# One operation of 2048 columns in place of two of 1024 on VectorE, in the expert stage of a two-layer transformer block

## The chip, the cores and the metric

The kernel runs on one core of one Trainium2 chip. The metric is the device time of one execution in microseconds (us). All products are made on the matmul engine (PE); VectorE is called DVE, ScalarE ACT, GpSimd POOL and SyncE SP. PEld is PE's weight load, a track of its own in the trace.

## The reference

Two transformer layers run one after the other on 256 tokens of width 2048. The stage of interest is the second layer's `peer`: each token picks 16 of 16384 experts in each of 8 heads, takes the product of its input with each chosen row of a first table (`expert_u`), and adds up the rows of a second table (`expert_v`) with the resulting weights.

```python
    kk = PEER_HEADS * PEER_TOPK
    xt = xn.reshape(nblk, PEER_TOK_BLOCK, D)
    it = eidx.reshape(nblk, PEER_TOK_BLOCK, kk)
    gt = gates.reshape(nblk, PEER_TOK_BLOCK, kk)

    def block(args):
        xb, ib, gb = args
        act = jax.nn.gelu(jnp.einsum('tkd,td->tk', expert_u[ib], xb))
        return jnp.einsum('tk,tkd->td', act * gb, expert_v[ib])
```

## The kernel before

**How the stage computes.** The kernel does most tokens densely: 224 of the 256 tokens are multiplied by all 16384 rows of both tables, and the weights of the experts that a token didn't choose are zero. The other 32 tokens (`ROWS`) fetch their chosen rows. For each of 32 numbers c, one indirect DMA of POOL (`gather`, L2187) brings 128 rows of the first table into one of three buffers `rows`, and DVE multiplies them by the tokens and sums (the list `SUM`, L2516). Later 32 more gathers bring rows of the second table, and DVE adds them, each times its weight, into `row_sum` (the list `ADD`, L2527 for c = 0 and L2529 after that; `row_sum` and `row_tokens` in the trace are one tensor).

**Pieces and steps.** Weights arrive as pieces of 128x2048 fp32 (1 MB). PE multiplies in fp32r, so each piece is split into a rounded part, `weights_hi`, and the rest that the rounding left, `weights_lo`. ACT makes `weights_hi` in two halves of 128x1024 (`split_hi`, L188), and DVE makes `weights_lo` as the piece minus `weights_hi` (`split_lo`, L195), likewise in two halves, each of which waits for its own half of `weights_hi`. PE starts a piece when all of its `weights_lo` is there (`ring.wait`). There are two buffers each of `weights_hi` and `weights_lo`, so ACT may start on piece n when PE has finished piece n - 2, that is, while PE works on piece n - 1. The raw pieces lie in four slots. SP fills a slot (L148) when DVE has finished the `weights_lo` of the piece that was in it.

The stage counts its pieces as steps s. Steps 0 to 15 are the query weights, 16 to 143 the first table (PE lines L2231 and L2232), 144 to 271 the second table (L2286 and L2287), and 16 further steps belong to the matrix after it. `V0` is 144. Below, "step V0+33" is the step in which ACT and DVE split the piece 33 of the second table. Each engine walks through the steps in a program order written out by hand. In a step s from V0 on, DVE does, in this order:

- `weights_lo` of piece s;
- a row operation, if s is in `ADD`;
- `normed` times the tokens' scale (L2535, 128x1792), in the two steps of each 16 ahead of those in the list `CURVE`;
- eight evacuations of PE's sums (`leave_sums`, L2469), every 8th step. ACT has copied the other half of each (`spill_sums`, L2347) just before;
- the addition of these sums to the residual (`add_sums`, L2478), every 8th step;
- a subtraction of the list `SPLIT` (L2552, 128x448), after ACT's copy of the same list (L2410);
- a product of the list `PROD` (L2560, 128x448).

`SPLIT` and `PROD` are made of offsets within a group of 16 steps; both have an entry at V0+16g+1 and at V0+16g+13. PE begins the first piece of every eight (V0+8k) only when `leave_sums` has emptied the first bank, and goes on bank by bank.

**The row operations before.** Each gathered row set is handled in two halves of 1024 columns, in two different steps. `SUM` holds the 64 steps 78 to 141, and `ADD` 64 steps from V0+17 on that leave out the offsets 0, 5, 6, 8, 10 and 14 of each 16. The gather that reuses a buffer waits until both halves are done (`row_summed`).

Of the kernel before, what the change touches and what calls it, by code (L numbers as in the profile page):

```python
# [6 lines left out]
F32 = mybir.dt.float32  # L7
# [3 lines left out]
ALU = mybir.AluOpType  # L11
# [6 lines left out]
D = 2048  # L18
# [88 lines left out]
class Ring:  # L107
# [82 lines left out]
    def split_lo(self, dve, stream, i, j, half, skip=0):  # L190

        hi, lo, raw = self.piece(self.hi, half, stream), self.piece(self.lo, half, stream), self.raw(j, half, stream)
        for part, (k, n) in enumerate(self.parts_of(stream)):
            dve.wait_ge(self.hi_ready, i * 16 + (2 * (2 * (self.fills + j) + half) + part + 1))
            last = dve.tensor_tensor(lo[:, k, n], raw[:, k, n], hi[:, k, n].bitcast(F32), ALU.subtract)  # L195
        last.then_inc(self.lo_ready, 1 + skip)

# [29 lines left out]
class Kernel:  # L227
    WQ, ROWS, ZEROED = 384, 32, 8
# [1687 lines left out]
    def peer(self, stream):  # L1916
        nc, a, ring = self.nc, self.a, self.ring
        U0, V0, END = PQ_TILES, PQ_TILES + NKEYS, PQ_TILES + 2 * NKEYS
# [3 lines left out]
        ROWS, BUFS = self.ROWS, 3  # L1922
        SUM = [*range(78, 142)]
        DOTS = SUM[-1] + 1
        free = [s for s in range(V0 + 17, V0 + 118) if (s - V0) % 16 not in (0, 5, 6, 8, 10, 14)]
        ADD = [free[k * len(free) // (2 * ROWS)] for k in range(2 * ROWS)]
# [31 lines left out]
        with ExitStack() as ctx:  # L1958
# [41 lines left out]
            row_sum = xg  # L2000
# [134 lines left out]
            with self.block() as block:  # L2135
# [306 lines left out]
                def _(dve):  # L2442
# [40 lines left out]
                    for s in range(END):  # L2483
# [3 lines left out]
                        ring.split_lo(dve, tiles, i, j, half)  # L2487
# [23 lines left out]
                        for k in [k for k, at_step in enumerate(SUM) if at_step == s]:  # L2511
                            c, part = divmod(k, 2)
                            if part == 0:
                                dve.wait_ge(gathered[c % BUFS], 16 * (c // BUFS + 1))
                            row, x_row = [y[:, part * D // 2:(part + 1) * D // 2] for y in (rows[:, c % BUFS, :], xg)]
                            dve.tensor_tensor_reduce(row, row, x_row, 1.0, 0.0, ALU.mult, ALU.add, dots[:, part, c:c + 1])\  # L2516
                                .then_inc(row_summed, 1)
                        for k in [k for k, at_step in enumerate(ADD) if at_step == s]:
                            c, part = divmod(k, 2)
                            if part == 0:  # L2520
                                dve.wait_ge(gathered[(ROWS + c) % BUFS], 16 * ((ROWS + c) // BUFS + 1))
                            row, to = [y[:, part * D // 2:(part + 1) * D // 2] for y in (rows[:, (ROWS + c) % BUFS, :], row_sum)]
                            weight = row_gate[:, 0, c:c + 1]
                            if c > 0 or part > 0:
                                dve.wait_ge(row_summed, 2 * ROWS + max(k - 1, 0))
                            if c == 0:
                                last = dve.tensor_scalar(to, row, weight, None, ALU.mult)  # L2527
                            else:
                                last = dve.scalar_tensor_tensor(out=to, in0=row, scalar=weight, in1=to, op0=ALU.mult, op1=ALU.add)  # L2529
                            last.then_inc(row_summed, 1)  # L2530
# [6 lines left out]
                        if s == DOTS:  # L2537
                            dve.wait_ge(row_summed, 2 * ROWS)
                            dve.tensor_tensor(row_gate[:, 1, :], dots[:, 0, :], dots[:, 1, :], ALU.add).then_inc(row_scores, 1)
# [527 lines left out]
```

## Time and profile before

| what | value |
|---|---|
| median of 3 runs | 2959.6 us (2958.5 to 2960.16) |
| the profiled execution's own time | 2959.44 us |
| its span in the trace | 2957.7 us |
| PE busy | 2910.0 us, 98% |
| DVE busy | 1969.9 us, 67% |
| ACT busy | 1388.9 us, 47% |
| POOL busy | 593.0 us, 20% |
| granted PE clock | 0.998 of full |

The span is the profiler's, from the first to the last instruction; the execution's own time is 1.7 us longer. The busy share of an engine is a mean over stages with different loads: the table above doesn't tell which engine another one waits for. The profile's lists of waits and its timelines do.

### The profile page before, as it was taken

To read this page: it belongs to the slowest core of one execution; us is meant where nothing else is said; L and a number is where in the kernel's file an instruction comes from. 1 tells how busy PE (TensorE), PEld (TensorE's weight loads), DVE (VectorE), ACT (ScalarE), POOL (GpSimd) and SP (SyncE) were. 2 spreads that over 40 slices of the span, in tenths; PEclk is the share of its full clock that TensorE was granted. 3 is DMA by queue.
4 is the path that set the end of the run, shared out by engine and by line. 5 is a ranking of instruction groups with operands and counts; after the bars stand their busy time and mean duration, and the time that the engine had idled before them with its cause. 6 is when DMAs were issued, how large, how long until landed. Compare 5 with 4: busy or idle time off the path is not lost.

```text
span 2957.7 us, 41749 instructions
## 1 busy us (share of the span) xinstructions
PE 2910.0 (98%) x16599; PEld 2625.5 (89%) x16599; DVE 1969.9 (67%) x2753; ACT 1388.9 (47%) x1992; POOL 593.0 (20%) x555
## 2 busy tenths in 40 slices
PE   8999999999999999999999999999999999999999
PEld 7998778888888887978789999999999999999999
DVE  5556654444444445464568999677787888888876
ACT  4355544444444444354444444444455555555553
POOL 2000000000000000150004888488710000000000
PEclk9999999999999999999999999999999999999999
DMA  8554356666665554544567888899997888888764
GB/s 292 162 168 151 115 175 222 224 234 231 226 197 183 187 198 140 176 153 156 177 218 252 226 224 224 279 328 336 343 375 266 314 324 323 324 316 316 260 215 141
DMA packets 244456, 692.88 MB, mean 234 GB/s; under 512 B 46569, under 2 KB 98825, under 8 KB 210880
## 3 DMA queue, kind: packets, MB, share of 16 engines
q1 hardware_dynamic: 194560, 600.81, 59.4%
q0 software_dynamic: 47168, 86.54, 10.5%
q10 hardware_dynamic: 2560, 3.21, 0.4%
q8 instruction: 115, 1.88, 0.3%
q14 instruction: 53, 0.43, 0.0%
HBM read 654.70 MB, written 33.69 MB: 233 GB/s over the span
## 4 chain that ended last, share of the span: by engine, by line
PE 49%; DVE 2%; ACT 0%; issue 0%; ACTq 0%; DVEq 0%
PE banks L2231 16%; PE banks L2286 15%; PE banks L2232 8%; PE banks L2287 7%; PE banks L2307 1%; PE banks L2309 1%; PE banks L2308 1%; DVE weights_lo L195 1%; PE banks L2250 0%; DVE peer_features L376 0%; DVE top_index L2049 0%; ACT weights_hi L188 0%; PE banks L2259 0%; PE banks L2275 0%; DVE row_gates L2063 0%
## 5 line engine op out<-in xcount | busy, mean ns | idle before, releaser
L195 DVE TENSOR_TENSOR weights_lo<-weights,weights_hi 128x1024 fp32r<-128x1024 f32 (+4 forms) x1080 | 1228.4, 1179 | 702.8 <-ACT weights_hi L188 700.7
L188 ACT ACTIVATE weights_hi<-weights 128x1024 fp32r<-128x1024 f32 (+4 forms) x1080 | 1046.5, 1017 | 1370.6 <-PE banks L417 639.7
L2231 PE MATMUL banks<-peer_features,weights_hi 128*128 128x448 f32 (+1 forms) x2304 | 734.8, 378 | 6.1 <-DVE weights_lo L195 6.1
L415 PE MATMUL banks<-weights_hi,features_hi 128*128 128x512 f32 (+3 forms) x1600 | 608.0, 380 | 26.2 <-DVE weights_lo L195 23.0
L2232 PE MATMUL banks<-peer_features,weights_lo 128*128 128x224 f32 (+1 forms) x2304 | 610.2, 265 | 0.0
L417 PE MATMUL banks<-weights_hi,features_lo 128*128 128x512 f32 (+3 forms) x1600 | 602.5, 377 | 0.0
L416 PE MATMUL banks<-weights_lo,features_hi 128*128 128x512 f32 (+3 forms) x1600 | 602.4, 377 | 0.0
L2286 PE MATMUL banks<-peer_features,weights_hi 128*128 128x448 f32 x1568 | 492.5, 374 | 0.0
L2231 PEld LDWEIGHTS banks<-peer_features,weights_hi 128*128 128x128 f32 x2304 | 432.0, 187 | 48.6 <-DVE weights_lo L195 8.7
L2232 PEld LDWEIGHTS banks<-peer_features,weights_lo 128*128 128x128 f32 x2304 | 439.2, 191 | 0.0
L2197 POOL DMA_INDIRECT expert_gates<-peer_choice x224 | 399.4, 1783 | 182.3 <-DVEq L2071 102.8
L2287 PE MATMUL banks<-peer_features,weights_lo 128*128 128x224 f32 x1568 | 414.6, 264 | 0.0
L415 PEld LDWEIGHTS banks<-weights_hi,features_hi 128*128 128x128 f32 x1600 | 302.6, 189 | 76.3 <-issue 25.3
L416 PEld LDWEIGHTS banks<-weights_lo,features_hi 128*128 128x128 f32 x1600 | 303.1, 189 | 44.8 <-issue 0.2
L417 PEld LDWEIGHTS banks<-weights_hi,features_lo 128*128 128x128 f32 x1600 | 302.4, 189 | 45.3
L2286 PEld LDWEIGHTS banks<-peer_features,weights_hi 128*128 128x128 f32 x1568 | 294.2, 188 | 22.0
L2287 PEld LDWEIGHTS banks<-peer_features,weights_lo 128*128 128x128 f32 x1568 | 299.7, 191 | 0.0
L268 POOL TENSOR_SCALAR statistics<-statistics 128x2 f32<-128x2 f32 (+3 forms) x16 | 6.8, 428 | 799.3 <-DVE statistics L393 502.7
L2286 PE MATMUL banks<-applied_parts,weights_hi 128*128 128x448 f32 x480 | 152.7, 374 | 0.0
L2187 POOL DMA_INDIRECT expert_rows<-in_expert_v,attention_statistics x32 | 34.3, 1073 | 553.3 <-DVE row_tokens L2529 422.7
L415 PE MATMUL banks<-weights_hi,ffn_turned_hi 128*128 128x512 f32 x352 | 137.9, 392 | 0.0
L417 PE MATMUL banks<-weights_hi,ffn_turned_lo 128*128 128x512 f32 x352 | 137.4, 390 | 0.0
(400 smaller groups left out, 2729.3 us busy)
## 6 DMA issues: line engine op xcount, KB each, us to landing
weights<-in_expert_u SPq DMA_DIRECT2D x128, 1024.0 KB, 6.3
weights<-in_expert_v SPq DMA_DIRECT2D x128, 1024.0 KB, 6.4
weights<-in_w_ffn_gate SPq DMA_DIRECT2D x44, 1024.0 KB, 5.2
weights<-in_w_ffn_up SPq DMA_DIRECT2D x44, 1024.0 KB, 5.2
weights<-in_w_ffn_down SPq DMA_DIRECT2D x44, 1024.0 KB, 4.8
weights<-in_w_in SPq DMA_DIRECT2D x48, 900.0 KB, 5.0
weights<-in_w_out SPq DMA_DIRECT2D x32, 1024.0 KB, 5.1
weights<-in_w_in SPq DMA_DIRECT2D x24, 704.0 KB, 4.2
```

The lines of the kernel that those rows point to most:

```text
L188: act.activation(hi[:, k, n], raw[:, k, n], ACT.Copy).then_inc(self.hi_ready, 1 + skip)
L195: last = dve.tensor_tensor(lo[:, k, n], raw[:, k, n], hi[:, k, n].bitcast(F32), ALU.subtract)
L415: pe.matmul(out, xh, wh, start=first, stop=False)
L416: pe.matmul(out, xh, wl, start=False, stop=False)
L417: return pe.matmul(out, xl, wh, start=False, stop=last_one)
L2187: pool.indirect_dma_start(out=rows[:, c % BUFS, :], out_offset=None, in_=rows_d if c < ROWS else values_d, in_offset=bass.IndirectOffsetOn ...
L2197: pool.indirect_dma_start(out=g_rows[:, :], in_=gates_of[:, t, slot:slot + 1], in_offset=None, compute_op=ALU.add, out_offset=bass.Indirec ...
L2231: pe.matmul(self.bank(n % 3, 2 * cols), wh[:, k, :], F[:, k, :, 0:cols], start=(k == 0), stop=False)
L2232: last = pe.matmul(self.bank(n % 3, cols), wl[:, k, :], F[:, k, 0, 0:cols], start=False, stop=(k == KD - 1))
L2286: pe.matmul(both, wh[:, e, cols], applied_pair[:, e], start=(pair == 0 and e == 0), stop=False)
L2287: last = pe.matmul(self.bank(c, DENSE), wl[:, e, cols], applied_pair[:, e, 0], start=False, stop=(pair == 7 and e == 1))
L2307: pe.matmul(out, wh[:, k, cols], F[:, kk, 0, :], start=(kk == 0), stop=False)
```

## The change

Three things change, all on DVE, and nothing else in the program:

- From V0 on, `weights_lo` is made in one operation of 128x2048 (`split_lo_whole`), which waits for both halves of `weights_hi`. The steps before V0, and the 16 steps after the second table, keep the two halves.
- Each gathered row set is handled in one operation of 2048 columns. `SUM` is now every second step from 78 to 140. `ADD` has 32 steps, those in which the first halves stood. The semaphore `row_summed` counts two for each operation, so POOL's gathers wait for the same numbers.
- The partial dot products are no longer two to be added; a copy stands where the addition was.

```diff
+    def split_lo_whole(self, dve, stream, i, j, half):
+
+        hi, lo, raw = self.piece(self.hi, half, stream), self.piece(self.lo, half, stream), self.raw(j, half, stream)
+        dve.wait_ge(self.hi_ready, i * 16 + (2 * (2 * (self.fills + j) + half) + 2))
+        dve.tensor_tensor(lo, raw, hi.bitcast(F32), ALU.subtract).then_inc(self.lo_ready, 1)
...
-        SUM = [*range(78, 142)]
-        DOTS = SUM[-1] + 1
+        SUM = [*range(78, 142, 2)]
+        DOTS = SUM[-1] + 2
         free = [s for s in range(V0 + 17, V0 + 118) if (s - V0) % 16 not in (0, 5, 6, 8, 10, 14)]
-        ADD = [free[k * len(free) // (2 * ROWS)] for k in range(2 * ROWS)]
+        ADD = [free[k * len(free) // ROWS] for k in range(ROWS)]
...
-                        ring.split_lo(dve, tiles, i, j, half)
+                        if s < V0:
+                            ring.split_lo(dve, tiles, i, j, half)
+                        else:
+                            ring.split_lo_whole(dve, tiles, i, j, half)
...
+                        for c in [c for c, at_step in enumerate(SUM) if at_step == s]:
+                            dve.wait_ge(gathered[c % BUFS], 16 * (c // BUFS + 1))
+                            row = rows[:, c % BUFS, :]
+                            dve.tensor_tensor_reduce(row, row, xg[:, :], 1.0, 0.0, ALU.mult, ALU.add, dots[:, 0, c:c + 1])\
+                                .then_inc(row_summed, 2)
+                        for c in [c for c, at_step in enumerate(ADD) if at_step == s]:
+                            dve.wait_ge(gathered[(ROWS + c) % BUFS], 16 * ((ROWS + c) // BUFS + 1))
+                            row, weight = rows[:, (ROWS + c) % BUFS, :], row_gate[:, 0, c:c + 1]
+                            dve.wait_ge(row_summed, 2 * (ROWS + c))
                             if c == 0:
-                                last = dve.tensor_scalar(to, row, weight, None, ALU.mult)
+                                last = dve.tensor_scalar(row_sum[:, :], row, weight, None, ALU.mult)
                             else:
-                                last = dve.scalar_tensor_tensor(out=to, in0=row, scalar=weight, in1=to, op0=ALU.mult, op1=ALU.add)
-                            last.then_inc(row_summed, 1)
+                                last = dve.scalar_tensor_tensor(out=row_sum[:, :], in0=row, scalar=weight, in1=row_sum[:, :],
+                                                                op0=ALU.mult, op1=ALU.add)
+                            last.then_inc(row_summed, 2)
...
-                            dve.tensor_tensor(row_gate[:, 1, :], dots[:, 0, :], dots[:, 1, :], ALU.add).then_inc(row_scores, 1)
+                            dve.tensor_copy(row_gate[:, 1, :], dots[:, 0, :]).then_inc(row_scores, 1)
```

With the edited formula, `ADD` holds these offsets from V0: 17, 19, 23, 27, 29, 33, 35, 39, 43, 45, 49, 51, 55, 59, 61, 65, 67, 71, 75, 77, 81, 83, 87, 91, 93, 97, 99, 103, 107, 109, 113 and 115. Seven of them are of the form 16g+1 and six of the form 16g+13.

The order of DVE's instructions from the `weights_lo` of step V0+32 to that of step V0+35, in the kernel before:

```order
L195 TENSOR_TENSOR weights_lo<-weights,weights_hi 128x1024 x2
L2469 TENSOR_TENSOR peer_scratch<-banks,peer_scratch 128x224 x8
L195 TENSOR_TENSOR weights_lo<-weights,weights_hi 128x1024 x2
L2529 SCALAR_TENSOR_TENSOR row_tokens<-expert_rows,row_gates,row_tokens 128x1024
L2552 TENSOR_TENSOR peer_features<-normed,peer_features 128x2x224
L2560 TENSOR_TENSOR normed<-normed,peer_scratch 128x448
L195 TENSOR_TENSOR weights_lo<-weights,weights_hi 128x1024 x2
L2529 SCALAR_TENSOR_TENSOR row_tokens<-expert_rows,row_gates,row_tokens 128x1024
L2552 TENSOR_TENSOR peer_features<-normed,peer_features 128x2x224
L195 TENSOR_TENSOR weights_lo<-weights,weights_hi 128x1024 x2
```

The same steps in the changed kernel (lines are up to seven further down; L202 is `split_lo_whole`, L2532 the row operation):

```order
L202 TENSOR_TENSOR weights_lo<-weights,weights_hi 128x2048
L2475 TENSOR_TENSOR peer_scratch<-banks,peer_scratch 128x224 x8
L202 TENSOR_TENSOR weights_lo<-weights,weights_hi 128x2048
L2532 SCALAR_TENSOR_TENSOR row_tokens<-expert_rows,row_gates,row_tokens 128x2048
L2556 TENSOR_TENSOR peer_features<-normed,peer_features 128x2x224
L2564 TENSOR_TENSOR normed<-normed,peer_scratch 128x448
L202 TENSOR_TENSOR weights_lo<-weights,weights_hi 128x2048
L2556 TENSOR_TENSOR peer_features<-normed,peer_features 128x2x224
L202 TENSOR_TENSOR weights_lo<-weights,weights_hi 128x2048
```

Step V0+33 had a row operation of 1024 columns and step V0+34 another; now step V0+33 has one of 2048 ahead of its two small operations, and step V0+34 none.

The second place is the `weights_lo` of step V0+45 and what follows it, of the form 16g+13. Before:

```order
L195 TENSOR_TENSOR weights_lo<-weights,weights_hi 128x1024 x2
L2529 SCALAR_TENSOR_TENSOR row_tokens<-expert_rows,row_gates,row_tokens 128x1024
L2552 TENSOR_TENSOR applied_parts<-normed,applied_parts 128x2x224
L2560 TENSOR_TENSOR normed<-normed,peer_scratch 128x448
L195 TENSOR_TENSOR weights_lo<-weights,weights_hi 128x1024 x2
```

And in the changed kernel:

```order
L202 TENSOR_TENSOR weights_lo<-weights,weights_hi 128x2048
L2532 SCALAR_TENSOR_TENSOR row_tokens<-expert_rows,row_gates,row_tokens 128x2048
L2556 TENSOR_TENSOR applied_parts<-normed,applied_parts 128x2x224
L2564 TENSOR_TENSOR normed<-normed,peer_scratch 128x448
L202 TENSOR_TENSOR weights_lo<-weights,weights_hi 128x2048
```

The same four or five pieces of work follow each other; what was 1024 columns wide in the row operation is 2048 wide, and the next `weights_lo` stands behind it.

## Rows read from the trace of the kernel before

**Rows 1.** The page: busy time of each engine, granted PE clock by fortieth.

```profile
PE 2910.0 (98%) x16599; PEld 2625.5 (89%) x16599; DVE 1969.9 (67%) x2753; ACT 1388.9 (47%) x1992; POOL 593.0 (20%) x555
PEclk9999999999999999999999999999999999999999
```

**Rows 2.** What PE waited for, whole span: us in total, times, longest.

```profile
PE banks L415 <- DVE weights_lo L195: 23.0, 11, 12.0
PE banks L2231 <- DVE weights_lo L195: 6.1, 6, 1.6
```

**Rows 3.** Stretches: length; busy us (instructions) of PE, PEld, DVE, ACT, POOL; clock; DMA.

```profile
1700.00:1800.00 100.00, 98.96 (x635) 94.11 (x634) 92.21 (x235) 44.87 (x63) 85.37 (x49) 1.00 0.88 227
2000.00:2100.00 100.00, 100.00 (x640) 95.42 (x639) 75.85 (x101) 44.71 (x61) 84.80 (x50) 1.00 1.06 346
2400.00:2500.00 100.00, 100.00 (x639) 95.48 (x638) 88.35 (x100) 55.71 (x76) 5.39 (x5) 1.00 0.89 329
2213.00:2855.00 642.00, 642.00 (x4100) 612.87 (x4099) 536.21 (x598) 344.58 (x459) 31.24 (x29) 1.00 0.83 297
```

**Rows 4.** DVE's groups by shape, 1475 to 2958: busy us, mean ns | idle before.

```profile
L195 DVE TENSOR_TENSOR weights_lo<-weights,weights_hi 128x1024 fp32r<-128x1024 f32 x572 | 675.4, 1222 | 255.9 <-ACT weights_hi L188 254.5
L2529 DVE SCALAR_TENSOR_TENSOR row_tokens<-expert_rows,row_gates,row_tokens 128x1024 f32<-128x1024 f32 x62 | 79.3, 1279 | 0.0
L2516 DVE CUSTOM_DVE_ANT_0 expert_rows<-expert_rows,row_tokens 128x1024 f32<-128x1024 f32 x64 | 77.6, 1213 | 0.0
...
L2509 DVE TENSOR_TENSOR row_tokens<-row_tokens,expert_rows 128x2048 f32<-128x2048 f32 x1 | 2.3, 2295 | 0.0
L2478 DVE TENSOR_TENSOR residual<-residual,peer_scratch 128x2048 f32<-128x2048 f32 x1 | 2.3, 2286 | 0.0
```

**Rows 5.** Timeline of ACT, steps V0+32 to V0+34: start, us, instruction, [idle before].

```profile
2369.49 2.01 ACT L188 ACTIVATE weights_hi<-weights 128x1024 fp32r<-128x1024 f32 x2 [2.54 <-PE banks L2287]
...
2374.70 2.00 ACT L188 ACTIVATE weights_hi<-weights 128x1024 fp32r<-128x1024 f32 x2
...
2379.51 2.01 ACT L188 ACTIVATE weights_hi<-weights 128x1024 fp32r<-128x1024 f32 x2 [2.35 <-PE banks L2287]
```

**Rows 6.** Timeline of DVE, the same steps.

```profile
2370.58 2.36 DVE L195 TENSOR_TENSOR weights_lo<-weights,weights_hi 128x1024 fp32r<-128x1024 f32 x2 [0.38 <-ACT weights_hi L188]
2372.86 2.47 DVE L2469 TENSOR_TENSOR peer_scratch<-banks,peer_scratch 128x224 f32<-128x224 f32 x8
2375.78 2.36 DVE L195 TENSOR_TENSOR weights_lo<-weights,weights_hi 128x1024 fp32r<-128x1024 f32 x2 [0.45 <-ACT weights_hi L188]
2378.05 1.28 DVE L2529 SCALAR_TENSOR_TENSOR row_tokens<-expert_rows,row_gates,row_tokens 128x1024 f32<-128x1024 f32 x1
2379.25 0.62 DVE L2552 TENSOR_TENSOR peer_features<-normed,peer_features 128x448 fp32r<-128x448 f32 x1
2379.78 0.62 DVE L2560 TENSOR_TENSOR normed<-normed,peer_scratch 128x448 f32<-128x448 f32 x1
```

**Rows 7.** Timeline where PE waited for `weights_lo` in the first table.

```profile
1664.53 2.36 DVE L195 TENSOR_TENSOR weights_lo<-weights,weights_hi 128x1024 fp32r<-128x1024 f32 x2
...
1665.41 0.19 PEld L2231 LDWEIGHTS banks<-peer_features,weights_hi 128*128 128x128 f32 x1
...
1665.52 0.19 PEld L2232 LDWEIGHTS banks<-peer_features,weights_lo 128*128 128x128 f32 x1
...
1666.08 2.01 ACT L188 ACTIVATE weights_hi<-weights 128x1024 fp32r<-128x1024 f32 x2 [2.76 <-PE banks L2232]
...
1666.94 0.19 PEld L2231 LDWEIGHTS banks<-peer_features,weights_hi 128*128 128x128 f32 x1 [1.23 <-DVE weights_lo L195]
```

**Rows 8.** Timeline of SP, then of DVE, around the latest load of scores.

```profile
2629.65 0.49 SPq L2158 DMA_DIRECT2D normed<-expert_scores  x1
...
2636.81 2.36 DVE L195 TENSOR_TENSOR weights_lo<-weights,weights_hi 128x1024 fp32r<-128x1024 f32 x2 [0.92 <-ACT weights_hi L188]
2641.22 2.03 DVE L2535 TENSOR_TENSOR normed<-normed,peer_rstd 128x1792 f32<-128x1792 f32 x1 [2.06 <-DMA normed<-expert_scores]
2643.17 2.35 DVE L195 TENSOR_TENSOR weights_lo<-weights,weights_hi 128x1024 fp32r<-128x1024 f32 x2
```

**Rows 9.** Waits of POOL from 1900, of SP from 2213; landing of second-table pieces.

```profile
POOL expert_rows L2187 <- DVE row_tokens L2529: 422.7, 28, 24.5
POOL expert_rows L2187 <- DVE row_products L2516: 42.8, 5, 9.1
...
SPq L148 <- DVE weights_lo L195: 579.4, 128, 6.4
...
weights<-in_expert_v SPq DMA_DIRECT2D x128, 1024.0 KB, 6.4
```

More of the change, by code:

```diff
@@ L2510, in _ @@
                             dve.sem_inc(xg_made, 1)
[L2511 to L2525, printed above, removed]
+                        for c in [c for c, at_step in enumerate(SUM) if at_step == s]:
[3 more added lines that the diff above has]
+                                .then_inc(row_summed, 2)
```

## The prediction

> **What bounds the kernel now.** I read the page first: PE is busy for 98% of the span at full clock, and no other engine is above 67% [rows 1]. A busy share doesn't say who waits, so the list of PE's waits came next. In the whole span PE waited 23.0 us in the earlier layers (L415) and 6.1 us in the expert stage (L2231) [rows 2]. No wait stands at the second table's lines (L2286, L2287). The windows say the same: from 2213 to 2855 us PE is busy 642.00 of 642.00 us, and DVE 536.21 [rows 3]. So in the stage that the change edits most there is no PE time to win. The question is only whether PE starts to wait.
>
> For that I need each step's clock. In ACT's timeline the two halves of `weights_hi` start at 2369.49, 2374.70 and 2379.51; two steps are 10.02, one is 5.01 us [rows 5]. The middle one is 0.20 late, because ACT has the eight evacuations ahead of it. I write all times below as offsets from the regular start of ACT's halves in a step.
>
> - Both halves of `weights_hi` are there at +2.01 [rows 5].
> - DVE's first half starts 1.09 to 1.10 after ACT's first (2370.58 against 2369.49), where one half takes about 1.05: a handoff of 0.04. Two halves take 2.36, and DVE's next instruction starts 2.28 after them (2372.86) [rows 6]. So `weights_lo` is ready at 1.09 + 2.36 = +3.45.
> - When does PE want it? The one stall shown answers. PE's last two loads of a piece start at 1665.41 and 1665.52, and pairs of loads come every 0.31, so it wanted the next at 1665.72. ACT's next halves started at 1666.08, when that piece was finished. PE wants a piece 0.36 before ACT starts on the next but one: at 5.01 - 0.36 = +4.65. DVE ended at 1664.53 + 2.36 = 1666.89 and PE loaded at 1666.94: a handoff of 0.05 [rows 7].
>
> The slack now is 4.65 - 0.05 - 3.45 = 1.15 us a step.
>
> **The change, part by part.**
>
> *One operation for `weights_lo`, 128 steps.* 128x2048 fp32 operations of this kind take 2.29 in the rows there are, against 1.222 for 1024 [rows 4]; I take 2.29, and 2.21 to the next start (the same 0.08 of overlap as in [rows 6]). It may start only after both halves: +2.01 + 0.04 = +2.05, and ends at +4.34. With the handoff it is +4.39 against +4.65: slack falls from 1.15 to 0.26 us, and no stall by itself. In the steps V0+8k+1 ACT is 0.20 late, so it is +4.59: still in time by 0.06. In the steps V0+8k there is one more: `leave_sums` comes 2.21 after +2.05, its first evacuation ends 0.38 later (eight take 2.47 [rows 6], so some 0.30 from start to start and a tail of 0.08), and PE wants that bank at once: 2.05 + 2.21 + 0.38 + 0.05 = +4.69 against +4.65. That is 0.04 for 15 such steps: **0.6 us**.
>
> *One row operation in the second table, 32 steps.* 1024 columns take 1.279 [rows 4] and 1.20 to the next start (2378.05 to 2379.25 [rows 6]). No row shows 2048 of this form. Below, it is bounded by the plain operation's 2.21; above, by two halves, 2.40. I take 1.20 + 1.06 = 2.26, with the slope of [rows 4] (2.286 - 1.222). A step with `weights_lo`, the row operation, a `SPLIT` and a `PROD` (0.53 to 0.54 each, start to start, [rows 6]) then holds 2.21 + 2.26 + 0.54 + 0.54 = 5.55 us of DVE's work, where a step is 5.01. Before it held 2.28 + 1.20 + 1.08 = 4.56.
>
> What is late next is the following `weights_lo`, which is queued behind it on DVE. After the seven steps V0+16g+1 of the list the sum is: start at 0.20 + 2.05, + 5.55 = 7.80, less 5.01 = +2.79 in the next step; ready at 2.79 + 2.29 + 0.05 = +5.13 against +4.65: 0.48 of PE's time, 7 x 0.48 = **3.4 us**. After the six steps V0+16g+13: 2.05 + 5.55 - 5.01 = +2.59, ready at +4.93: 0.28, 6 x 0.28 = **1.7 us**. The other 19 row operations stand with a `PROD` alone or less: 2.21 + 2.26 + 0.54 = 5.01, which fits. The step behind a late one holds no row operation, so the lateness dies there. PE's stall doesn't move ACT's next start by itself, as that hangs on the piece before.
>
> *Row operations in the first table.* There the two halves of `weights_lo` stay, so slack is 1.15. With `SUM` in every step DVE is busy 75.85 us in 100 [rows 3], about 20 steps: 3.8 a step. With twice 1024 columns a step holds about 5.1, the next 2.5. The `weights_lo` behind it starts at 1.09 + 5.1 - 5.01 = +1.2, and may start at 4.65 - 0.05 - 2.36 = +2.24. Cost 0; the cover is a whole microsecond. The copy in place of the addition of 32 columns is nothing either.
>
> *Queues.* Row buffers come free up to a step sooner, but POOL's gathers already waited 422.7 us for DVE in the second table [rows 9], with no wait of DVE for them. SP fills a raw slot 0.89 later, for a use four steps, 20 us, on; the landing takes 6.4 [rows 9]. Both 0. One transfer has no cover: in the latest case the load of scores, issued at 2629.65, let DVE go on only at 2641.22 [rows 8]. SP issues it behind a fill that waits for `weights_lo`, so it comes 0.89 later. That step's `weights_lo` starts at 2636.81, that is +1.09, so the load ends at +5.50, then +6.39; 1.95 of L2535 (2643.17 - 2641.22) makes +8.34, +3.33 in the next step, ready at +5.67: 1.0 us once. The traffic around it moves too, so I leave it out of the sum and put it in the range.
>
> Sum: 0.6 + 3.4 + 1.7 = 5.7, less some overlap of the small terms (a stall of 0.28 or 0.48 gives the following steps room; I take 0.2 off): 5.5. The profiled execution has 2959.44, so **2964.9 us**. That the median of the runs is 2959.6, 0.16 higher, changes nothing.
>
> The Trainium skill has two rules for this. "Perfetto Trace Analysis", section "Optimizing Scalar/DVE Operations", says that grouping operations helps if the engine is saturated, and that where it is not saturated but makes bubbles elsewhere, breaking them up lets work finish sooner. DVE is at 84% here (536.21 of 642 [rows 3]) and PE has no bubble, so the first rule would give 2959.4, no change; the second, read backwards, speaks against the change and gives my sum.
>
> **The rivals.**
>
> *No change.* DVE's real lateness stays under the slack, by some 0.3 less than I sum. For it: before, PE never waited here though DVE stood 88% busy [rows 3]. Against it: 5.55 is over 5.01 in 13 steps, and only 0.26 is left. Time 2959.5.
>
> *Every handoff a little worse.* If whole operations end 0.1 later than I take (2.36 busy, or a longer handoff after the second half), the 28 stalls grow by 0.1 each: +2.8, 2967.7. With 0.2 it is 2970.5. From 0.26 on all 128 steps stall, and each further 0.1 costs 12.8. The load adds 1.0. For it: slack of 0.06 and of -0.04 in two of eight steps.
>
> *Faster.* It would need PE's own pace to rise with fewer DVE instructions. PE makes 640 matmuls in 100 us with DVE at 75.85, and 639 with DVE at 88.35 [rows 3]; in the older window 635 in 98.96, the same pace, with DVE at 92.21. So the pace doesn't hang on DVE. It decides from a pace 1% quicker (6.4 us of 642): 2953.
>
> **How the numbers follow.** About 0.2% (5.9 us) is what a measurement of this kernel can tell from no change. Forecast, stalls at the 28 named places, 2962 to 2968: 0.62, of which 0.24 lies above 2965.5. No change: 0.14. Every handoff worse: 0.20. Faster: 0.04. Range: 2959.0, the no-change case, to 2971.5, the worse handoff of 0.2 with the load; what is left out is the rest of that rival and the faster one. Within 0.2%: 0.38 + 0.14 = 0.52. Slower: 0.24 + 0.20 = 0.44. Faster: 0.04.
>
> **What would show it right or wrong.** PE's list of waits has a new row at the second table's matmuls, released by `weights_lo`, with about 13 waits of 0.2 to 0.5 us and possibly 15 tiny ones, 5 to 6 us in all. 128x2048 `weights_lo` takes 2.29 and starts 2.05 after ACT's first half. The 2048-column row operation takes 2.35. DVE's idle time before `weights_lo` roughly doubles where it is not late. If PE waits at all 128 pieces, the slack was mis-sized; if nowhere, the handoffs were. A wait at the first table's lines beyond the 6.1 us would show that the row operations there are not covered.

## The result, and the profile after

The changed kernel takes 2965.55 us (median of 13 runs, 2964.32 to 2967.47) against 2959.68 for the kernel before (13 runs beside it): ratio 1.0022, 95% interval 1.0014 to 1.0029. It is 5.9 us slower. The forecast was 2964.9.

The page of the changed kernel, busy time of each engine and granted clock:

```profile
PE 2914.9 (98%) x16599; PEld 2625.1 (89%) x16599; DVE 1951.8 (66%) x2529; ACT 1391.5 (47%) x1992; POOL 602.0 (20%) x555
PEclk9999999999999999999999999999999999999999
```

DVE has 224 instructions fewer and is 18 us less busy than in [rows 1]. The time went up all the same. The window from 2213 to 2855 answers to the last row of [rows 3]. Here it is for the changed kernel, then its list of PE's waits over the whole span (us in total, times, longest):

```profile
2213.00:2855.00 642.00, 640.30 (x4064) 606.95 (x4063) 519.01 (x438) 345.50 (x459) 31.29 (x29) 1.00 0.83 295
```

```profile
PE banks L421 <- DVE weights_lo L195: 21.9, 10, 11.9
PE banks L2237 <- DVE weights_lo L195: 5.4, 6, 1.6
...
PE banks L2292 <- DVE weights_lo L202: 1.3, 7, 0.2
...
PE banks L2292 <- DVE peer_scores L2461: 0.4, 1, 0.4
```

L421 and L2237 are the lines of [rows 2], as before. L2292 is the second table (L2286 before), and it is new in this list. The list shows only 1.7 us there, because the profile models a matmul's end and can so cover a short stall. The weight loads (PEld) start at regular distances, so gaps between their starts show it better. The group of loads that holds both the first and the last load of the second table, before and then after, with what ended the idle time of PE and PEld at this line in the changed kernel:

```profile
L2286 PEld LDWEIGHTS banks<-applied_parts,weights_hi x480: 186/189/193, 2213.4 to 2859.8; 128*128 128x128 f32 x160
```

```profile
L2292 PEld LDWEIGHTS banks<-applied_parts,weights_hi x480: 186/189/192, 2212.5 to 2864.7; 128*128 128x128 f32 x160
...
  DVE weights_lo L202: 3.1, 13
  issue: 2.5, 6
  DVE peer_scores L2461: 1.0, 2
```

The stretch of the second table is 2859.8 - 2213.4 = 646.4 us before and 2864.7 - 2212.5 = 652.2 after: +5.8. The rest of the difference in these two traces (the stage starts 0.9 sooner after) lies ahead of anything that the change touches in the first table, and comes and goes from trace to trace.

Where are the 5.8 us? Loads come in pairs: the two of a pair start 0.11 apart, and the next pair 0.20 to 0.21 after that. I took every distance above 0.24 in the PEld timeline and subtracted 0.21:

| place | gaps | each, us | sum |
|---|---|---|---|
| first piece, the last of its eight chunks | 1 | 0.63 | 0.6 |
| first piece of each eight, V0+8k | 15 | 0.05 to 0.10 | 1.3 |
| V0+16g+2, from V0+34 on | 6 | 0.40 to 0.43 | 2.4 |
| V0+16g+14, from V0+30 on | 6 | 0.17 to 0.50 | 1.6 |

That is 6.0, unrounded, and there are no other gaps that the kernel before doesn't have. It has one that the changed kernel doesn't, at V0+86, behind the late load of [rows 8]. PE's loads there, before:

```profile
2645.22 0.19 PEld L2287 LDWEIGHTS banks<-applied_parts,weights_lo 128*128 128x128 f32 x1
2645.64 0.19 PEld L2286 LDWEIGHTS banks<-applied_parts,weights_hi 128*128 128x128 f32 x1 [0.23 <-issue]
```

0.42 less 0.21 is 0.21, and 6.0 less 0.2 is the 5.8 of the stretch. (Two distances of 1.99, at V0+118 and V0+126, stand in both kernels: there PE loads `row_sum` for 16 matmuls of another line.) How one of the new gaps comes about can be read from the steps V0+32 to V0+34, the same as in [rows 5, 6]. DVE of the changed kernel:

```profile
2371.80 2.29 DVE L202 TENSOR_TENSOR weights_lo<-weights,weights_hi 128x2048 fp32r<-128x2048 f32 x1 [1.90 <-ACT weights_hi L188]
2374.01 2.47 DVE L2475 TENSOR_TENSOR peer_scratch<-banks,peer_scratch 128x224 f32<-128x224 f32 x8
2376.99 2.29 DVE L202 TENSOR_TENSOR weights_lo<-weights,weights_hi 128x2048 fp32r<-128x2048 f32 x1 [0.52 <-ACT weights_hi L188]
2379.20 2.35 DVE L2532 SCALAR_TENSOR_TENSOR row_tokens<-expert_rows,row_gates,row_tokens 128x2048 f32<-128x2048 f32 x1
2381.46 0.62 DVE L2556 TENSOR_TENSOR peer_features<-normed,peer_features 128x448 fp32r<-128x448 f32 x1
2382.00 0.62 DVE L2564 TENSOR_TENSOR normed<-normed,peer_scratch 128x448 f32<-128x448 f32 x1
2382.53 2.29 DVE L202 TENSOR_TENSOR weights_lo<-weights,weights_hi 128x2048 fp32r<-128x2048 f32 x1
```

ACT of the changed kernel in steps V0+33 and V0+34, and PE's loads around the start of piece V0+34:

```profile
2374.96 2.00 ACT L188 ACTIVATE weights_hi<-weights 128x1024 fp32r<-128x1024 f32 x2
...
2379.88 2.01 ACT L188 ACTIVATE weights_hi<-weights 128x1024 fp32r<-128x1024 f32 x2 [2.46 <-PE banks L2293]
```

```profile
2384.33 0.19 PEld L2293 LDWEIGHTS banks<-peer_features,weights_lo 128*128 128x128 f32 x1
2384.94 0.19 PEld L2292 LDWEIGHTS banks<-applied_parts,weights_hi 128*128 128x128 f32 x1 [0.42 <-issue]
```

The last `weights_lo` has no idle time ahead of it: both halves of its `weights_hi` were there at 2379.88 + 2.01 = 2381.89, but DVE came at 2382.53. It ended at 2384.82, PE wanted it at 2384.33 + 0.21 = 2384.54 and loaded at 2384.94. The three shapes of DVE that the forecast had to take from other operations, busy us and mean ns:

```profile
L202 DVE TENSOR_TENSOR weights_lo<-weights,weights_hi 128x2048 fp32r<-128x2048 f32 x128 | 293.4, 2292 | 125.4 <-ACT weights_hi L188 125.4
L2523 DVE CUSTOM_DVE_ANT_0 expert_rows<-expert_rows,row_tokens 128x2048 f32<-128x2048 f32 x32 | 73.0, 2281 | 0.0
L2532 DVE SCALAR_TENSOR_TENSOR row_tokens<-expert_rows,row_gates,row_tokens 128x2048 f32<-128x2048 f32 x31 | 72.7, 2346 | 0.0
```

### The profile page after: what moved, and what is told of

The parts are those of the page before. It is cut to its first block, busy times and chain, and to the rows that moved or that the text cites. A ratio compares the mean times of both kernels' runs of the same rounds, so it can differ in the third digit from the quotient of the medians.

```text
span 2962.6 us, 41558 instructions
## 1 busy us (share of the span) xinstructions
PE 2914.9 (98%) x16599; PEld 2625.1 (89%) x16599; DVE 1951.8 (66%) x2529; ACT 1391.5 (47%) x1992; POOL 602.0 (20%) x555
## 4 chain that ended last, share of the span: by engine, by line
PE 46%; DVE 3%; issue 1%; ACT 1%; ACTq 0%; DVEq 0%
PE banks L2237 16%; PE banks L2292 13%; PE banks L2238 8%; PE banks L2293 6%; PE banks L2313 1%; PE banks L2315 1%; PE banks L2314 1%; DVE weights_lo L195 1%; ACT weights_hi L188 1%; DVE row_tokens L2532 1%; DVE weights_lo L202 1%; PE banks L2256 0%; DVE peer_features L382 0%; DVE top_index L2055 0%; DVE normed L2564 0%
## 5 line engine op out<-in xcount | busy, mean ns | idle before, releaser
L195 DVE TENSOR_TENSOR weights_lo<-weights,weights_hi 128x1024 fp32r<-128x1024 f32 (+4 forms) x824 | 926.3, 1166 | 603.4 <-ACT weights_hi L188 576.4
L2237 PE MATMUL banks<-peer_features,weights_hi 128*128 128x448 f32 (+1 forms) x2304 | 735.2, 378 | 5.4 <-DVE weights_lo L195 5.4
L421 PE MATMUL banks<-weights_hi,features_hi 128*128 128x512 f32 (+3 forms) x1600 | 607.3, 380 | 25.1 <-DVE weights_lo L195 21.9
L2292 PE MATMUL banks<-peer_features,weights_hi 128*128 128x448 f32 x1568 | 494.9, 375 | 1.2 <-DVE weights_lo L202 1.2
L2237 PEld LDWEIGHTS banks<-peer_features,weights_hi 128*128 128x128 f32 x2304 | 431.7, 187 | 48.4 <-DVE weights_lo L195 8.1
L2203 POOL DMA_INDIRECT expert_gates<-peer_choice x224 | 416.8, 1861 | 180.7 <-DVEq L2077 103.2
L202 DVE TENSOR_TENSOR weights_lo<-weights,weights_hi 128x2048 fp32r<-128x2048 f32 x128 | 293.4, 2292 | 125.4 <-ACT weights_hi L188 125.4
L421 PEld LDWEIGHTS banks<-weights_hi,features_hi 128*128 128x128 f32 x1600 | 302.0, 189 | 75.2 <-issue 24.1
L2292 PEld LDWEIGHTS banks<-peer_features,weights_hi 128*128 128x128 f32 x1568 | 294.0, 188 | 26.8 <-issue 2.1
L2292 PE MATMUL banks<-applied_parts,weights_hi 128*128 128x448 f32 x480 | 153.0, 374 | 0.5 <-DVE peer_scores L2461 0.4
L421 PE MATMUL banks<-weights_hi,ffn_turned_hi 128*128 128x512 f32 x352 | 137.9, 392 | 0.0
```

The costliest lines, as they stand in the source:

```text
L202: dve.tensor_tensor(lo, raw, hi.bitcast(F32), ALU.subtract).then_inc(self.lo_ready, 1)
L421: pe.matmul(out, xh, wh, start=first, stop=False)
L2203: pool.indirect_dma_start(out=g_rows[:, :], in_=gates_of[:, t, slot:slot + 1], in_offset=None, compute_op=ALU.add, out_offset=bass.Indirec ...
L2237: pe.matmul(self.bank(n % 3, 2 * cols), wh[:, k, :], F[:, k, :, 0:cols], start=(k == 0), stop=False)
L2292: pe.matmul(both, wh[:, e, cols], applied_pair[:, e], start=(pair == 0 and e == 0), stop=False)
```

## The experiments

Theory A is that of the forecast: an operation on both halves makes `weights_lo` ready 0.9 us later, and a row operation of double width makes some steps longer than PE's; only both together make PE wait for long. Rival B blames the row operations, rival C the wide `weights_lo` as such. "Stretch" in the table is from PE's first to its last load of the second table, as above.

| kernel | median us | ratio, 95% interval | stretch, against 646.4 |
|---|---|---|---|
| the change | 2965.55 | 1.0022 (1.0014 to 1.0029) | +5.8 |
| e1, only `weights_lo` whole | 2961.53 | 1.0007 (0.9998 to 1.0016) | +2.1 |
| e2, only rows whole | 2959.87 | 1.0001 (0.9992 to 1.0010) | -0.1 |
| e3, halves that wait for both | 2968.72 | 1.0032 (1.0020 to 1.0044) | +8.4 |
| e4, rows moved | 2975.32 | 1.0047 (1.0033 to 1.0061) | +16.7 |
| e5, e4 and entries in halves | 2970.25 | 1.0040 (1.0026 to 1.0054) | +10.4 |
| e6, halves in crowded steps | 2961.80 | 1.0008 (0.9999 to 1.0017) | +1.0 |
| e7, halves in late steps | 2966.34 | 1.0024 (1.0015 to 1.0034) | +6.6 |
| e8, a delay in each step | 2988.89 | 1.0101 (1.0086 to 1.0117) | +29.4 |
| e9, whole in part of the first table | 2962.53 | 1.0008 (0.9999 to 1.0017) | -0.1 |
| e10, halves where it is tight | 2960.93 | 1.0005 (0.9996 to 1.0014) | +0.7 |
| e11, e5 with an earlier load | 2960.07 | 1.0001 (0.9992 to 1.0010) | +0.6 |

The single runs of e1, e6, e9, e10 and e11 spread over 3 to 6 us, and the interval of each holds 1. So for these the stretch and the gaps in it, each from one trace, say more than the time.

### One part alone: e1 and e2

e1 is the kernel before with this edit alone:

```diff
-                        ring.split_lo(dve, tiles, i, j, half)
+                        if s < V0:
+                            ring.split_lo(dve, tiles, i, j, half)
+                        else:
+                            ring.split_lo_whole(dve, tiles, i, j, half)
```

> Only the weights_lo of the second table in one operation; the row operations stay in halves of 1024. Theory A (each weights_lo comes 0.9 later because it waits for both halves of weights_hi, and PE waits where DVE's work of a step then runs past the next step): the crowded steps hold one half row operation, 4.5 us of work, so the gaps of 0.2 to 0.4 us at pieces 16g+2 and 16g+14 vanish; what stays is the gap at the first piece (0.6) and the one of 0.1 in each eighth piece, about 2 us in all: 2961 to 2962. Rival B (the row operations of 2048 columns are what costs, by blocking DVE or by their gathers): 2959.6, no gap. Rival C (one operation for weights_lo costs by itself): the whole loss stays, 2965.5.

e2 is the changed kernel with `weights_lo` in halves everywhere (`if s < V0` becomes `if s < END`).

> Only the row operations in 2048 columns, in both tables; weights_lo in halves everywhere. Theory A: DVE starts weights_lo at +1.1 in a step, a crowded step ends by +6.7, which is +1.7 in the next, and +2.2 would still do: no gap in PE's loads, 2959.6 within 1 us. Rival B: the whole loss, 2965.5. Rival C: 2959.6 as well.

In e1 the gap at the first piece (0.62) and the fifteen of 0.1 stay. Of the twelve larger ones none stays at its old place. A single gap of 0.36 stands at piece V0+70, behind a load of scores for which DVE waited 1.43 us: the late load of [rows 8], at another place. In e2 no gap of the change is left. PE's loads in e2:

```profile
L2292 PEld LDWEIGHTS banks<-applied_parts,weights_hi x480: 187/189/192, 2212.4 to 2858.7; 128*128 128x128 f32 x160
```

646.3 us: the row operations of 2048 columns cost nothing by themselves, in either table. B falls with e2. C, by which the whole loss stays, falls with e1, which has 2.1 of the 5.8. The remaining 3.7 need both edits.

### Start or width: e3

```diff
-        dve.tensor_tensor(lo, raw, hi.bitcast(F32), ALU.subtract).then_inc(self.lo_ready, 1)
+        for k, n in self.parts_of(stream):
+            last = dve.tensor_tensor(lo[:, k, n], raw[:, k, n], hi[:, k, n].bitcast(F32), ALU.subtract)
+        last.then_inc(self.lo_ready, 1)
```

> As the changed kernel, but weights_lo of the second table in two operations of 1024, of which the first already waits for both halves of weights_hi. Theory A: what costs is the later start, not the width; the pair takes 2.36 and 2.28 to the next start where one takes 2.29 and 2.21, so each gap grows by 0.07 (28 gaps, +2 us): 2967 to 2968. Rival C (the width itself costs): back to 2959.6.

2968.72, and every gap grew: 0.37 to 0.43 where 0.30 stood, 0.67 to 0.71 where 0.61 stood (spacing included). The halves with the late wait are worse than one operation, by 2.6 us in the stretch. So the width as such is a gain of some 0.07 us an operation, and the loss lies in the start.

### Another place for the row operations: e4, e5 and e11

e4 puts the 32 row operations where no product and subtraction stand together:

```diff
-        free = [s for s in range(V0 + 17, V0 + 118) if (s - V0) % 16 not in (0, 5, 6, 8, 10, 14)]
+        free = [s for s in range(V0 + 17, V0 + 118) if (s - V0) % 16 in (2, 3, 4, 7, 11)]
```

> As the changed kernel, but the 32 row operations of the second table stand at offsets 2, 3, 4, 7 and 11 of each 16 steps, where no step has both a product and a subtraction of the gates beside them. Theory A: no step holds more than 5.0 us of DVE's work, so the 12 gaps at pieces 16g+2 and 16g+14 (4.1 us with their usual spacing taken off) vanish, and those of 0.1 and the first of 0.6 stay: 2961 to 2962. Rival C: 2965.5, since nothing about weights_lo changed. Rival B: 2965.5 too, as the operations are as wide and as many.

The expectation of 2961 to 2962 failed: 2975.32. The twelve gaps did vanish, but six others came, once in 16 steps: five of 1.9 to 2.7 us and one of 0.44, 11.7 in all (spacing taken off). DVE's waits for transfers in the second table, in e4, and its timeline at one of them:

```profile
DVE normed L2539 <- DMA normed<-expert_scores: 17.8, 6, 3.7
```

```profile
2565.78 2.29 DVE L202 TENSOR_TENSOR weights_lo<-weights,weights_hi 128x2048 fp32r<-128x2048 f32 x1
2571.01 2.02 DVE L2539 TENSOR_TENSOR normed<-normed,peer_rstd 128x1792 f32<-128x1792 f32 x1 [2.94 <-DMA normed<-expert_scores]
2572.96 2.29 DVE L202 TENSOR_TENSOR weights_lo<-weights,weights_hi 128x2048 fp32r<-128x2048 f32 x1
```

DVE stands 2.94 us at the load of scores, and the next `weights_lo`, queued behind it, is late by as much. This is the late load of [rows 8], here in six places. With the gaps of 0.1 and the first (1.9) this makes 13.6 of the 16.7 us. The rest is PE's clock. In the windows right behind the first of these gaps and behind the fifth, it was granted only the lower of its two levels, 1.2 of 2.4 GHz, for 3.4 us each:

```profile
2328.60:2332.20 3.60, 3.60 (x15) 3.32 (x14) 3.60 (x3) 0.15 (x1) 0.00 (x0) 0.53 0.93 355
...
2741.80:2745.40 3.60, 3.60 (x15) 3.34 (x14) 3.60 (x3) 0.38 (x1) 0.00 (x0) 0.53 1.02 398
```

15 matmuls in 3.60 us, where 23 would be the usual (640 in 100 us, [rows 3]): 1.3 to 1.7 us lost each time. PE had stood idle for 2.7 and 2.0 us just before.

With three row operations in neighbouring steps, three gathers of 1 MB go out one step apart, just around this load. POOL's gathers and SP's load in e4, ahead of the wait shown above:

```profile
2555.56 1.08 POOL L2193 DMA_INDIRECT expert_rows<-in_expert_v,attention_statistics  x1 [34.18 <-DVE row_tokens L2532]
2560.57 1.08 POOL L2193 DMA_INDIRECT expert_rows<-in_expert_v,attention_statistics  x1 [3.94 <-DVE row_tokens L2532]
2565.59 1.08 POOL L2193 DMA_INDIRECT expert_rows<-in_expert_v,attention_statistics  x1 [3.94 <-DVE row_tokens L2532]
```

```profile
2558.55 0.44 SPq L2164 DMA_DIRECT2D normed<-expert_scores  x1
```

The load is issued at 2558.55 and DVE goes on at 2571.01, 12.5 us later. The landing times of the loads into `normed` in that stretch (min, median, max), in e4 and in the changed kernel:

```profile
DMA to landing us min/median/max: 8.3/12.5/13.6
```

```profile
DMA to landing us min/median/max: 8.3/8.8/11.8
```

e5 adds halves in 17 steps to e4:

```diff
-                        if s < V0:
+                        if s < V0 + 2 or (s - V0) % 8 == 0:
```

> As e4, and weights_lo in halves again in the first two steps of the second table and in every eighth after that, 17 of 128. Theory A: the gap of 0.6 at the first piece comes from the last sum of the first table, which DVE takes out only behind the weights_lo of the second piece; the gaps of 0.1 come from the first bank's evacuation behind a later weights_lo. Both vanish: 2959.6 to 2960.5, with 111 of 128 pieces still in one operation. If the gaps stay, their cause is another.

2970.25, where 2959.6 to 2960.5 was expected. The gap at the first piece vanished and so did those of 0.1 (two of 0.05 to 0.10 are left), but five of the six at the load stayed (0.9 to 2.8 us), with 15.2 us of DVE's waits for it. e11 then moves only the load, in e5:

```diff
-            LOADS |= {V0 // 2 + 8 * g + k: 2 * g + i for k, i in ((3, 2), (5, 3))}
+            LOADS |= {V0 // 2 + 8 * g + k: 2 * g + i for k, i in ((2, 2), (5, 3))}
```

> As e5, with the load of scores and of gates that DVE needs at offset 5 of each 16 steps issued two steps (10 us) sooner. In e4 and e5 PE waited 1 to 3 us once in each 16 steps: DVE stood at this load with weights_lo behind it, and three gathers of 1 MB, one step apart, went out just around the load. If the load's late landing is the cause, the six gaps vanish: 2959.6 to 2960.5. If it is something else about three row operations in a row, they stay, near 2970.

2960.07, DVE doesn't wait for the load at all, and the gaps at it are gone. Landing in e11:

```profile
DMA to landing us min/median/max: 8.4/8.6/9.6
```

So the load's landing was the cause in e4 and e5, not the density of DVE's work. That the gathers around it are what made it land late fits the rows above, but no run moved the gathers without the row operations. What is left are six gaps of 0.07 to 0.15 at V0+24, V0+40 and so on, behind a step with a row operation.

### Which step must start early: e6 and e7

e6 gives the halves back to the crowded steps, e7 to the steps for whose pieces PE waited.

```diff
-                        if s < V0:
+                        if s < V0 or (s - V0) % 16 in (1, 13):
```

> As the changed kernel, but weights_lo in halves in the crowded steps themselves, offsets 1 and 13 of each 16. Theory A: DVE starts 0.95 earlier in these steps, so the weights_lo of the next step isn't late: the 12 gaps vanish, 2961 to 2962.

```diff
-                        if s < V0:
+                        if s < V0 or (s - V0) % 16 in (2, 14):
```

> As the changed kernel, but weights_lo in halves in the steps behind the crowded ones, offsets 2 and 14: just the pieces for which PE waited. Theory A: these are late because DVE comes late to them, and their weights_hi has long been there, so halves win nothing and cost 0.07 more: 2965.5 to 2967. A theory by which PE waits because this very operation waits for both halves of weights_hi expects the 12 gaps to vanish: 2961 to 2962.

DVE of e6, then of e7, at the same steps V0+33 and V0+34:

```profile
2375.51 2.35 DVE L195 TENSOR_TENSOR weights_lo<-weights,weights_hi 128x1024 fp32r<-128x1024 f32 x2
2377.77 2.34 DVE L2532 SCALAR_TENSOR_TENSOR row_tokens<-expert_rows,row_gates,row_tokens 128x2048 f32<-128x2048 f32 x1
...
2381.11 2.28 DVE L202 TENSOR_TENSOR weights_lo<-weights,weights_hi 128x2048 fp32r<-128x2048 f32 x1
```

```profile
2377.73 2.29 DVE L202 TENSOR_TENSOR weights_lo<-weights,weights_hi 128x2048 fp32r<-128x2048 f32 x1 [0.53 <-ACT weights_hi L188]
2379.94 2.35 DVE L2532 SCALAR_TENSOR_TENSOR row_tokens<-expert_rows,row_gates,row_tokens 128x2048 f32<-128x2048 f32 x1
...
2383.27 2.35 DVE L195 TENSOR_TENSOR weights_lo<-weights,weights_hi 128x1024 fp32r<-128x1024 f32 x2
```

In e6 the twelve gaps are gone (and the first one too, since V0+1 is among the steps). In e7 all twelve are there, each 0.06 to 0.09 wider. The piece that PE waits for isn't late through its own wait; it is late because `weights_lo` of the step ahead began late.

### How much slack there is: e8

e8 leaves the computation as it is and adds, ahead of each `weights_lo` of the second table, a sum whose result isn't used:

```diff
                         else:
+                            dve.wait_ge(ring.hi_ready, i * 16 + (2 * (2 * (ring.fills + j) + half) + 2))
+                            dve.tensor_reduce(pad[:, s % 4, :], self.ident[:, 0:96].unsqueeze(1).to_broadcast([P, 4, 96]), AX.X, ALU.add)
                             ring.split_lo_whole(dve, tiles, i, j, half)
```

> As the changed kernel, with one more operation ahead of each weights_lo of the second table (a sum over 384 columns of a constant, some 0.47 us, whose result nobody reads): a dose for the slack. Theory A has 0.26 us of slack in a plain step: PE waits 0.2 at most of the 128 pieces and more behind crowded steps, 25 to 40 us in all: 2985 to 3000. If the slack were 0.5 or more, plain pieces would show no gap and the time would stay below 2975.

The added operation in its trace (duration ns min/median/max), and what ended PE's idle time at the first matmul line of the second table:

```profile
L2498 DVE TENSOR_REDUCE delay<-identity x128: 539/553/555, 2209.4 to 2878.7; 128x4 f32<-128x384 f32 x128
```

```profile
  DVE weights_lo L202: 22.9, 48
  issue: 13.9, 31
```

2988.89. Its 0.553 less 0.08 of overlap is a delay of 0.47. Where plain steps follow each other (V0+2 to V0+6, V0+36 and V0+38, and so on) every second piece shows a gap of 0.21 to 0.25: 0.47 - 0.26 = 0.21 was expected from the slack of 0.26. (Every second, it seems, because a stall of PE gives the next step that much room.) Elsewhere there are also smaller gaps, from 0.03 on, in neighbouring pieces.

### The same edit where DVE is close to its limit: e9

e9 is the kernel before, with `weights_lo` whole in the steps 11 to 75 of the first table:

```diff
-                        ring.split_lo(dve, tiles, i, j, half)
+                        if not RET < s < 76:
+                            ring.split_lo(dve, tiles, i, j, half)
+                        else:
+                            ring.split_lo_whole(dve, tiles, i, j, half)
```

> The kernel before, with the weights_lo of the steps 11 to 75 in one operation: the steps of the first table in which DVE also chooses the experts, is over 90% busy, and PE waits for it 5 to 6 us in all. The second table stays in halves. Theory A: one operation ends 0.07 sooner only where DVE comes late, and starts 0.95 later where it doesn't; the lateness builds up over a few steps from one that begins on time, so PE's waits grow by up to 0.9 us each, 2961 to 2964. Rival (where DVE is near its limit, fewer and larger operations finish sooner): PE's waits there shrink by 0.2 to 0.3 us each, 2958.5 to 2959.5.

PE's waits in the first table, in e9, against 6.1 us in [rows 2]:

```profile
PE banks L2237 <- DVE weights_lo L202: 5.9, 4, 1.5
PE banks L2237 <- DVE weights_lo L195: 2.7, 2, 1.6
```

The four gaps in the steps that were changed are 1.93 to 1.95 us wide (spacing included), where the kernel before has 1.12, 1.43, 1.50 and 1.13. PE's stretch from its first to its last load for the query weights and the first table (L2231 before) is 751.7 us against 748.2, and 3.1 of these 3.5 lie in steps that were changed. DVE was busy 296.1 us instead of 303.1 in the window from 1527 to 1865, and PE waited longer. Theory A had the gaps grow by up to 0.9 us each, and they grew by 0.44 to 0.81; the rival had them shrink.

### Undoing it only where it hurts: e10

```diff
-                        if s < V0:
+                        if s < V0 + 2 or (s - V0) % 16 in (0, 1, 8, 13):
```

> The changed kernel, with weights_lo in halves in 33 of the 128 steps of the second table: the first two, every eighth, and the offsets 1 and 13 of each 16; the row operations stand where the change put them. Theory A: every gap that the change made has its cause in one of these steps, so none stays: 2959.6 within 1 us, with the gap of the first piece and the fifteen of 0.1 gone too.

2960.93, 0.3 above the expected range; 32 steps have halves, and not 33 as the expectation says. Of the change's gaps six are left, 0.07 to 0.15 us, at V0+24, V0+40 and so on: these pieces start behind a step with a row operation (offset 7). At V0+24 DVE comes to `weights_lo` at 2330.49, when both halves of `weights_hi` are there (2328.46 + 2.01 = 2330.47). So the halves win nothing and take 0.07 longer. That was not in the expectation, which had none; it comes to 0.7 us.

No version beats the kernel before. In the second table there is next to nothing to win: PE's loads have one gap there, the 0.21 us at V0+86.

## Why the prediction was right

**What bounds the kernel.** Right: PE had next to no idle time to give in the second table (0.2 us, which its list of waits doesn't show), DVE's 18 us of saved work bought nothing, and the whole change was in PE's new waits.

**One operation for `weights_lo`.** It takes 2.292 (2.29 was taken) and starts 2.03 us after ACT's first half (2376.99 - 2374.96; 2.05). The slack of 0.26 in a plain step holds by e8. The fifteen gaps at V0+8k came, at 0.05 to 0.10 each and not 0.04: 1.3 us, where 0.6 was forecast. The handoff accounts for it. DVE's first evacuation of step V0+32 starts at 2374.01 and takes 0.38, and PE's load follows at 2374.51, 0.12 after its end and not 0.05 as in [rows 7]. It is 0.12 at V0+34 too (2384.94 - 2384.82), but 0.05 at V0+30, V0+46 and so on. The pieces with 0.12 wait for at least one semaphore more than those with 0.05; that this is the reason was not tried. The 1.09 to 1.10 from ACT's start to DVE's is 1.08 to 1.09 in [rows 5, 6], which changes nothing. The rival of worse handoffs had all 128 steps stall once the slack is used up. In e8 it is used up, and PE's loads show 74 gaps; the delay cost 23.6 us (29.4 - 5.8), where 128 x 0.21 is 27.

**Row operations in the second table.** The width of 2.346 was right (2.35), the mechanism too, and e1, e2 and e6 show it. "The seven steps V0+16g+1" was one too many. The first row operation (c = 0, at V0+17) is no addition but a plain product, and it is far quicker. In the changed kernel:

```profile
L2530 DVE TENSOR_SCALAR row_tokens<-expert_rows,row_gates x1: 1281/1281/1281, 2298.4 to 2298.4; 128x2048 f32<-128x2048 f32 x1
```

Six gaps of 0.40 to 0.43 came, 2.4 us against 3.4. They are smaller than 0.48, and the gap at V0+8k, two pieces ahead, has its part in that: it pushes PE and so gives the step room. In each of the six places the two gaps add up to 0.49, whether they are 0.09 and 0.40 or 0.06 and 0.43. The longer handoff would add 0.07 to this, so the working is not exact to better than that. The six at V0+16g+14 gave 1.6 against 1.7, but not evenly. Five are 0.17 to 0.25, and V0+62 has 0.50: there ACT starts the step before 0.3 late, in the kernel before too, and the forecast took every such step to be on time.

**Missing from the sum.** The first piece, 0.6 us. PE begins it with banks 3 to 7. Banks 0 to 2 still hold the last scores of the first table and come at the end, each when DVE has taken these out. For the last of them DVE does so behind the `weights_lo` of step V0+1. PE's load there:

```profile
2217.57 0.19 PEld L2292 LDWEIGHTS banks<-applied_parts,weights_hi 128*128 128x128 f32 x1 [0.65 <-DVE peer_scores L2461]
```

In e2, e5, e6, e10 and e11, where V0+1 has halves, this gap is gone. The forecast named what is queued behind `weights_lo` for the steps V0+8k but not for this one.

**No cost.** The row operations of the first table: right, by e2. POOL's and SP's queues: right, DVE waits for no gather in the changed kernel. The late load, kept out of the sum and put at 1.0 us in the range, even gave back the 0.2 of V0+86 (DVE doesn't wait for it in the changed kernel). But it was the real danger of the place: e1 had one gap of 0.36 us, e4 six.

**The signs.** Two of those named did not come. PE's list of waits shows 8 new waits and 1.7 us, not about 13 and 5 to 6; the gaps between the loads show them. And DVE's idle time before `weights_lo` did not double: from 2213 to 2860 it went from 102.7 to 123.5 us.

**The sum.** 5.5 forecast, 5.8 in the stretch: +0.7 at V0+8k, +0.6 at the first piece, -1.0 and -0.1 at the two crowded places, +0.2 for the overlap, which is already in that -1.0, and -0.2 for the gap at V0+86 (the rest is rounding). So the closeness is in part luck: errors of +1.3 and -1.1 us cancelled.

The page "Perfetto Trace Analysis" of the Trainium skill says in "Optimizing Scalar/DVE Operations" that grouping can help a saturated engine, and that where an engine isn't saturated but makes bubbles on others, breaking up may let work finish sooner. e1 and e10 agree with the second half of this: one operation for `weights_lo` cost 2.1 us, and halves in 32 of the 128 steps brought the change's 5.8 down to 0.7. e3 shows its limit: halves that start no sooner cost 2.6 us more. e9 is against a plain reading of the first: at 303.1 of 338 us busy, DVE saved 7 us and PE's waits grew from 6.1 to 8.6.

## What to carry to other kernels

Ask of a merged operation not what it saves but when it may start: it waits for the last of its producers, and here that moved the end of `weights_lo` from 3.44 to 4.32 us after ACT's start (step V0+33), 0.88 later in a step of 5.01, for 0.07 saved. If it must merge, keep the halves in the step that *makes* DVE late, not in the step that is late (e6 against e7). And before moving work to a lighter step, look at what transfers it sets off and who stands on them (e4, e11).

## What the runs showed that was not expected

- A stall of PE is not passed on to ACT's next start, which hangs on the piece before: in the changed kernel ACT starts at 2379.88 and 2384.89, one step apart, though PE's load at 2384.94 came 0.40 late. So a fixed lateness makes PE wait at every second piece in plain steps (e8), and with the slack of 0.26 taken up first, 128 delays of 0.47 cost 23.6 us, not 60.
- With three gathers of 1 MB, one step of 5 us apart, around it, a load of 896 KB landed in 12.5 us in the median (e4), against 8.8 in the changed kernel, with the same transfers in all. Issued two steps sooner (e11) it took 8.6.
- After gaps of 2.7 and 2.0 us in e4 (but not after the others of 1.9 to 2.4), and after the longest of e5, 2.8 us, PE's clock was granted at half for 3.4 us, so these gaps cost more than their length.
- A row of waits can hide most of a loss: PE's list shows 1.7 us in the second table where the gaps between its loads add up to 6.0.
